# A fixed expert in the routed order of a mixture-of-experts layer, a narrow step moved to third place, and narrow steps that pair high and low ranks

## What is computed

```python
scores = jax.nn.sigmoid((hf @ router_w).astype(jnp.float32))
...
_, e_idx = lax.top_k(jnp.where(expert_mask, biased, -jnp.inf), TOP_K)   # 8 of 64 experts for each token
gate = jnp.take_along_axis(scores, e_idx, axis=1)
gate = gate / jnp.sum(gate, axis=-1, keepdims=True) * ROUTED_SCALE
...
def expert_block(args):
    xb, e = args
    return (jax.nn.silu(xb @ w_gate[e]) * (xb @ w_up[e])) @ w_down[e]    # 1024 -> 256 -> 1024
...
routed = jax.ops.segment_sum(yb * row_gate[:, None], row_tok, num_segments=T + 1)[:T]
```

## Time and profile before

| | us |
|---|---|
| median of three runs | 1796.85 (1791.96 to 1797.09) |
| the profiled execution | 1795.8 |
| its span, first to last instruction | 1794.0 |
| the routed steps within it, first gate and up matmul to the end of the last down products | 521 to 1025 |

### The profile page before, as it was taken

One profiled execution on the slowest core, in us unless ns is written; L12 is line 12 of the kernel. 1 busy time (PEld: TensorE's weight loads), 2 busy tenths in 40 slices (PEclk: granted clock), 3 DMA queues, 4 the chain that ended last, 5 costly groups with the idle time before them and its releaser, 6 DMA issues.

```text
span 1794.0 us, 31767 instructions
## 1 busy us (share of the span) xinstructions
PE 1726.1 (96%) x12878; PEld 1243.4 (69%) x12878; DVE 906.2 (51%) x1388; ACT 678.1 (38%) x987; POOL 303.4 (17%) x154
## 2 busy tenths in 40 slices
PE   6999999999999999999999999999998999999999
PEld 3899998789464444444443467788886679988887
DVE  4277851766862211221112377565447985576453
ACT  3444445733411211211111265454446542444432
POOL 1278877400000000000000000000000004410000
PEclk8999999999999999999999999999998999999999
DMA  9545543055789999999989933164544320025542
GB/s 382 188 166 187 188 177 129 1 218 205 305 347 386 421 408 421 409 371 423 421 349 406 418 134 119 71 238 178 211 164 173 132 94 27 4 97 186 210 165 93
DMA packets 52921, 413.67 MB, mean 231 GB/s; under 512 B 8481, under 2 KB 8513, under 8 KB 12464
## 3 DMA queue, kind: packets, MB, share of 16 engines
q1 hardware_dynamic: 45072, 391.14, 55.5%
q0 software_dynamic: 7296, 18.96, 2.8%
q10 hardware_dynamic: 416, 1.66, 0.2%
HBM read 548.94 MB, written 2.10 MB: 307 GB/s over the span
## 4 chain that ended last, share of the span: by engine, by line
PE 84%; DVE 9%; issue 2%; ACT 2%; POOL 0%; DVEq 0%; ACTq 0%; POOLq 0%
PE ps L1262 14%; PE ps L888 9%; PE ps L890 9%; PE ps L889 9%; PE ps L1281 7%; PE ps L950 5%; PE ps L952 5%; PE ps L951 5%; PE ps L1295 4%; PE ps L968 3%; PE ps L1698 3%; DVE ring_lo L2609 2%; PE ps L1248 2%; PE ps L998 1%; PE ps L1734 1%
## 5 line engine op out<-in xcount | busy, mean ns | idle before, releaser
L889 PE MATMUL ps<-ring_lo,arena_r 128*128 128x512 f32 x888 | 349.0, 393 | 0.0
L1262 PE MATMUL ps<-arena 128*32 128x512 f32 (+1 forms) x880 | 234.5, 598 | 1.2 <-issue 1.2
L888 PE MATMUL ps<-arena_r 128*128 128x512 f32 x560 | 224.1, 400 | 4.0 <-DVE ring_lo L2609 3.1
L890 PE MATMUL ps<-arena_r 128*128 128x512 f32 x560 | 219.9, 393 | 0.0
L952 PE MATMUL ps<-arena_r,ring_lo 128*128 128x256 f32 x768 | 217.3, 283 | 0.0
L1262 PE MATMUL ps<-ring,arena 128*32 128x512 f32 (+1 forms) x704 | 206.5, 596 | 1.2 <-issue 0.9
L2609 DVE TENSOR_TENSOR ring_lo<-ring,arena_r 128x2048 fp32r<-128x2048 f32 x69 | 157.3, 2290 | 78.3 <-ACT arena_r L1899 78.3
L889 PEld LDWEIGHTS ps<-ring_lo,arena_r 128*128 128x128 f32 x888 | 168.9, 190 | 33.4
L3109 DVE SCALAR_TENSOR_TENSOR arena<-ps,arena 128x256 f32<-128x256 f32 x36 | 17.4, 483 | 290.7 <-ACT arena L2076 290.6
L1899 ACT ACTIVATE high<-ring 128x2048 fp32r<-128x2048 f32 x59 | 112.8, 1913 | 111.4 <-PE ps L950 71.7
L950 PE MATMUL ps<-arena_r,high 128*128 128x256 f32 x528 | 151.0, 286 | 1.6 <-DVE ring_lo L2609 1.3
(11 more groups left out here) (507 smaller groups left out, 3378.2 us busy)
## 6 DMA issues: line engine op xcount, KB each, us to landing
ring<-in_weights SPq DMA_DIRECT2D x183, 1024.0 KB, 4.8
arena<-in_moe_gu SPq DMA_DIRECT2D x53, 2048.0 KB
ring<-in_moe_gu SPq DMA_DIRECT2D x34, 2048.0 KB
arena<-in_moe_dn SPq DMA_DIRECT2D x53, 1024.0 KB
ring<-in_moe_dn SPq DMA_DIRECT2D x34, 1024.0 KB
spare<-in_moe_gu SPq DMA_DIRECT2D x17, 2048.0 KB
twin<-in_moe_dn SPq DMA_DIRECT2D x17, 1024.0 KB
arena<-in_ln POOLq DMA_DIRECT2D x2, 1024.0 KB, 8.7
```

The source lines that it names most:

```text
L888: head = pe.matmul(dst, hi, w, start=start, stop=False, skip_group_check=True)
L889: pe.matmul(dst, hi, rest, start=False, stop=False, skip_group_check=True)
L890: return head, pe.matmul(dst, lo, w, start=False, stop=stop, skip_group_check=True)
L1262: mm = pe.matmul(pb("moe", mu("gu", i))[at, :], x_cols[:, k, at], gu_w[s % SETS][:, k * 512:(k + 1) * 512], start=(k == 0), stop=(k == KC ...
```

## The change

Expert 0 gets the last rank, 63, whatever its load; the others are ranked among themselves. Since its place is known, its weights are asked for without the ranking, ahead of all others, as unit 1 in set 1. Rank 63 belongs to the first narrow step, because the narrow step n now has ranks 40 + n and 63 - n. That step is moved from the seventh place in the order to the third. `weights_order` names the first six units, and gives the others to the sets in the order in which the steps free them.

```diff
-ORDER = [... for c in "SSSXXXZSXXZXZSZSZXSZZZSZXZXXXZZXXXXX"]
+ORDER = [... for c in "SSZSXXXSXXZXZSZSZXSZZZSZXZXXXZZXXXXX"]
+FIXED = (2, 1)
+FIXED_SET = 1
+FIXED_EXPERT, FIXED_ORDER = 0, EXPERTS - 1
...
-            "narrow": [quad + mixed + 2 * n, quad + mixed + 2 * n + 1, over + mixed + narrow + n, over + mixed + n]}[ORDER[i]]
+            "narrow": [quad + mixed + n, EXPERTS - 1 - n, over + mixed + narrow + n, over + mixed + n]}[ORDER[i]]
...
-    waiting = [(i, h) for i in range(STEPS) for h in range(len(sets_of(i)))]
-    order = []
+    first = [(0, 0), FIXED, (1, 0), (2, 0), (4, 0), (3, 0)]
+    order = dict(enumerate(first))
+    waiting = [(i, h) for i in range(STEPS) for h in range(len(sets_of(i))) if (i, h) not in first]
+    after = list(range(SETS))
     while waiting:
-        s = len(order)
-        fits = [(i, h) for i, h in waiting if (sets_of(i)[h] < EXPERTS if s < SETS else order[s - SETS][0] < i)]
-        order.append(fits[0])
-        waiting.remove(fits[0])
-    return order
+        s = min(after, key=lambda s: (order[s][0], s))
+        after.remove(s)
+        if s + SETS < W_UNITS:
+            fits = [(i, h) for i, h in waiting if order[s][0] < i]
+            order[s + SETS] = fits[0]
+            waiting.remove(fits[0])
+            after.append(s + SETS)
+    return [order[s] for s in range(W_UNITS)]
...
+            fixed_rows = slice(FIXED_EXPERT * P, FIXED_EXPERT * P + P)
+            sp.wait_ge(sem("x1_ready"), 1)
+            sp.dma_start(gu_w[FIXED_SET], a["moe_gu"][fixed_rows, :]).then_inc(sem(f"gu_in{FIXED_SET}"), 16)
+            sp.dma_start(dn_w[FIXED_SET], a["moe_dn"][fixed_rows, :]).then_inc(sem(f"dn_in{FIXED_SET}"), 16)
             sp.wait_ge(sem("tables"), 1)
-            sp.wait_ge(sem("x1_ready"), 1)
-            for s in (0, 1):
-                gate_up(s)
-                down(s)
+            gate_up(0)
+            down(0)
...
-            for s in (5, 3):
+            for s in (3, 5):
...
-                step(dve.tensor_reduce(order, larger, AX_X, A))
+                step(dve.tensor_reduce(order, larger[:, FIXED_EXPERT + 1:EXPERTS], AX_X, A))
+                step(dve.memset(order[FIXED_EXPERT:FIXED_EXPERT + 1, :], float(FIXED_ORDER)))
```

More of the change, by code:

```diff
@@ L121 @@
 SETS = 6
-ORDER = [{"S": "solo", "X": "mixed", "Z": "narrow"}[c] for c in "SSSXXXZSXXZXZSZSZXSZZZSZXZXXXZZXXXXX"]
+ORDER = [{"S": "solo", "X": "mixed", "Z": "narrow"}[c] for c in "SSZSXXXSXXZXZSZSZXSZZZSZXZXXXZZXXXXX"]
 UNUSED = float(1 << 20)
 CHIP_STEPS = 2
+FIXED = (2, 1)
+FIXED_SET = 1
+FIXED_EXPERT, FIXED_ORDER = 0, EXPERTS - 1
 def row_of(i):
```

## The result

The changed kernel takes **1801.14 us** (median of 6 runs, 1800.24 to 1806.27), the kernel before, measured beside it, 1794.11 (6 runs). The ratio is 1.0044, with a 95% interval of 1.0027 to 1.0062: slower by 7.0 us on the medians. The forecast was +7.2 us and 1804; the absolute number is 3 us high because it stands on the median of three runs, 1796.85, which six runs put at 1794.11.

The account below looks back on a forecast made before the run. Runs of steps with two filled units each were taken as bound by DMA, other steps by PE. 0 + 0.2 + 0 + 7.0 = +7.2 us on 1795.8 gives 1803.0, as a median 1804 us; range 1797 to 1810.

Parts of the forecast that it names:

- Part 1: Start of the routed steps: loading the fixed expert without the ranking gains a lead that is given back at once; 0.
- rival "faster": The early load's lead lives on to the tail, so the kernel is 7.4 us faster, 1789.4; chance 0.10.
- Part 2: In the ranking: one more VectorE instruction, between 0 and 0.2 us, taken as +0.2.
- Part 3: Narrow step moved to third place: between 0 and 1 us of wait at step 6, taken as 0.
- the two removed waits: PE's waits at 701.86 and 771.48 go, 3.36 us, so step 27 starts that much earlier.
- Part 4: New pairing of ranks: two early waits go, steps 27 to 35 run at DMA pace without a pause; +7.0 us.
- The clock adds nothing: Tail steps: slower matmuls at a lower clock go into the waiting; 0, with +2.8 us kept in the range.
- The end keeps its distance from step 35: Behind the routed steps: the end of the stage and all behind it shift with step 35; no further time.

Follow-up runs that it names:

- e3: The changed kernel with the fixed expert's two loads issued behind those of the first ranked unit, after the wait for the ranking; 1800.36 us, 1.0047 times before.
- c0: The changed kernel run again without an edit, beside the kernel before on the same chip; 1801.47 us, 1.0052 times before.
- e1: The kernel before with only the new pairing of ranks 40 + n and 63 - n; 1800.84 us, 1.0047 times before.
- e5: The changed kernel with the weights of step 8's two experts not loaded; 1801.97 us, 1.0038 times before.
- e7: The changed kernel with another order of steps, pairing kept, steps of two units spread more widely; 1800.25 us, 1.0023 times before.
- e6: The changed kernel with the row gathers of the last five steps cut to row 0 at most; 1795.59 us, 1.0011 times before.
- e2: The changed kernel with consecutive ranks in each narrow step but the first, both empty experts in step 30 again; 1794.16 us, 1.0008 times before.
- e4: The changed kernel with the weights of step 30's two experts not loaded; 1791.01 us, 0.9979 times before.

## Why the prediction was right, point by point

- **Part 1, the early load, 0:** right. The two DMAs stand on SP's queue at 476.65 and 477.13, the queue works in 492:500 and nearly rests in 515:522, and e3 finds no difference. The idle time is that of the prediction, since the second group is issued at 520.76 and not before. The rival "faster", a lead that lives on, is out.
- **Part 2, +0.2:** not to be seen. The first matmul came at 519.80, 1.25 us earlier than before, and c0, the same kernel, has it 2 us earlier still. The part ahead of the routed steps varies by more than this term from one execution to the next, so it stays open.
- **Part 3, the narrow step third, 0 out of "between 0 and 1":** the term that was mis-sized. The wait came where the prediction named it, for the weights of step 6, the third of the mixed steps: at 619.44, 1.01 us, at its down matmuls, which PE does between the gate and up matmuls of step 7 and those of step 8, and it is not taken back later: PE reaches the full stop of the queue near 790 that much later, and the tail begins later. By the matmuls' own starts step 8 is 1.2 us late in the first profile and 1.5 in c0, above the stated bound. The whole stage is 1.4 to 2.0 us longer in these two than in e1 and 0.5 longer in e5, which doesn't have this wait; those 0.5 are within what two profiles differ by. The order of the loads has a part in it. The down weights of step 6 are issued behind three filled gate and up loads, of step 7 and of step 8's two experts (SP's queue: start us, us, what it issues):

```profile
593.49 0.34 SPq L670 DMA_DIRECT2D ring<-in_moe_gu  x1
594.79 0.34 SPq L670 DMA_DIRECT2D arena<-in_moe_gu  x1
596.10 0.33 SPq L670 DMA_DIRECT2D ring<-in_moe_gu  x1
597.41 1.63 SPq L670 DMA_DIRECT2D arena<-in_moe_dn  x2
```

  e5 leaves out step 8's two, which step 6 doesn't need, and the wait is gone. It is the pattern of the long wait in e7, and the prediction's sum, which counts whole units, doesn't see it. The same argument that gave the credit for the two removed waits should have been used for the debt of the new one.
- **Part 4, the pairing, +7.0:** right; e1 alone has +6.7 in the stage. Its first half, step 27 starting 3.36 us earlier, is 365.1 us behind the first matmul in e1, and 886.2 - 521.05 = 365.15 in the prediction. Its second half, 125.0 us for the eight steps behind, is 125.03. The split within was off: 27 to 28 took 16.0, not 15.3, 32 to 33 took 15.42, not 16.01, and the last two 14.75, not 14.82. That these errors cancel to 0.1 us is luck. The gather in 27 to 28, of few rows, cost 1.2 us, as much as the full ones behind it, and the last one, in 32 to 33, only 0.6; in e6, gathers of one row at most are nearly free. How the price hangs on the rows isn't settled.
- **The clock adds nothing:** right for the stage. Twice the gate and up matmuls of a starved step ran in a stretch of lower clock (8.77 us in place of 7.07, at 902.75 and 950.87; granted clock 0.80 in 902.75:911.50), and the wait behind them shrank from 2.4 to 0.7, so the step still took 16.0. A wait as long (932.40, 2.42 us) was followed by full clock (1.00 in 934.80:941.90), so the prediction's step from a wait of 2.41 us to a slower clock is not the whole rule.
- **The end keeps its distance from step 35:** right as far as the change goes, but in single profiles it doesn't hold to the microsecond. From step 35's first matmul to the end the first profile has 786.7 us, before 789.8, and the other profiles 787.5 to 792.2. In the profiled pair this hides part of the loss (spans 1798.4 and 1794.0, +4.4, with +8.7 in the stage); the ratios over many runs don't have it. This is why the stage is compared above and not the span: the stage's differences from before (c0 +8.1, e1 +6.7, e2 +2.7, e4 -3.1, e6 +3.1, e7 +3.2) agree with the ratios (+9.3, +8.4, +1.4, -3.8, +2.0, +4.1 us) within 2 us each, and so do e3's and e5's (+8.0 and +7.2 against +8.4 and +6.8).

So the sum of +7.2 was made of a right +7.0 and a missing 1.4 to 2.0. The measured difference (7.0 on the medians, interval 4.8 to 11.1) can't tell the two sums apart; the traces do. That the medians give just 7.0 is luck too.

## What to carry to other kernels

Where loads run ahead of the compute by a fixed number of buffers, bytes have a place: two units saved ahead of a full stop of the queue were worth 1 to 1.5 us, and the same two in the stretch in which the queue never stops 11.2 of their 14.8 us. So before reordering, count the filled loads needed up to each step and ask whether the last long run of full steps loses its pause; balancing pairs by their load is the wrong aim when the pauses are what the tail lives on. An earlier issue earned nothing where the loads behind it weren't issued earlier as well. And the order of the loads counts, not only their number: twice PE waited for down weights that stood behind gate and up loads of later steps.

## What the runs showed of the hardware

- The granted clock of one and the same stretch behind the routed steps differs between executions, with nothing changed there. In 1440:1450 c0 has 1.00 and e5 0.67 (a mean between the levels of 2.4 and 1.2 GHz), PE being busy for all 10 us in both (windows of c0, then of e5):

```profile
1440.00:1450.00 10.00, 10.00 (x58) 8.24 (x57) 9.90 (x5) 0.20 (x1) 0.00 (x0) 1.00 0.00 0
```

```profile
1440.00:1450.00 10.00, 10.00 (x47) 8.46 (x46) 9.90 (x5) 0.00 (x0) 0.00 (x0) 0.67 0.00 0
```

  The first profile of the changed kernel, before and e7 have 0.83 there. The rest of the kernel behind step 35 took 787.8 us in c0 and 791.8 in e5. What decides over this clock wasn't looked into.
- A small indirect gather costs the weight stream up to 1.2 us of a starved step: 16.0 us with it, 14.8 without (e6); over e6's five gathers it is 1.0 on average. That is more than its 0.25 MB are at the stream's 425 GB/s, 0.6 us.
- A unit moved without a gather takes 7.4 us, 425 GB/s, whether the queue has been full for some 100 us (before, 889.59 to 904.41: 14.82 for two) or for more than 200 (the changed kernel, 997.04 to 1011.79: 14.75).
